# A decoder layer on one core: first stage with reordered weight loads and maxima, and the first chunk's input prepared in it

## The reference

```python
mod = silu(c) @ w_ada + b_ada                      # c: 9 rows (1 prompt, 8 samples); w_ada 1024 x 6144
sh1, sc1, g1, sh2, sc2, g2 = split(mod, 6)
h = rms_norm(x, norm1_w) * (1.0 + sc1) + sh1
proj = h @ w_in                                    # w_in 1024 x 4104
rq, rk, rv, rg, mq, mk, mv, mo, mi, mf = split(proj, ...)   # eight of 512 columns, two of 4
# retention over rq, rk, rv, gated by rg; mLSTM over mq, mk, mv, mo, mi, mf
x = x + g1 * (concat(y_r, y_m) @ w_out)
# then a second norm and a gated MLP with a causal convolution, and a last norm
```

## Time and profile before

| | |
|---|---|
| median of 3 runs | 2727.28 us (2724.01 to 2727.49) |
| the profiled execution's own time | 2726.41 us |
| its span | 2724.6 us |
| PE (TensorE matmul) busy | 2460.3 us, 90% |
| DVE (VectorE) busy | 1897.1 us, 70% |
| ACT (ScalarE) busy | 911.4 us, 33% |
| POOL (GpSimd) busy | 403.4 us, 15% |
| DMA | 279.87 MB, mean 103 GB/s |

### The profile page before, as it was taken

One profiled execution on the slowest core, in us unless ns is written; L12 is line 12 of the kernel. 1 busy time (PEld: TensorE's weight loads), 2 busy tenths in 40 slices (PEclk: granted clock), 3 DMA queues, 4 the chain that ended last, 5 costly groups with the idle time before them and its releaser, 6 DMA issues. The chain is left out here.

```text
span 2724.6 us, 44404 instructions
## 1 busy us (share of the span) xinstructions
PE 2460.3 (90%) x17028; PEld 1516.9 (56%) x17028; DVE 1897.1 (70%) x3889; ACT 911.4 (33%) x1371; POOL 403.4 (15%) x385
## 2 busy tenths in 40 slices
PE   2699999969999999599969999999999985899997
PEld 0355555557776777455536666666666652344443
DVE  6445565536888787568867777777777779967666
ACT  2324343314434444135432222222222224322222
POOL 0123222300000000012242212222122200000000
PEclk9999999979999999699989999999999997999999
DMA  9335434370242310433412221222122214333333
GB/s 258 105 112 163 149 122 135 102 247 33 86 147 85 141 71 15 131 117 111 134 50 73 79 74 49 75 76 74 61 66 72 78 63 159 112 94 103 107 89 93
DMA packets 197176, 279.87 MB, mean 103 GB/s; under 512 B 18840, under 2 KB 134088, under 8 KB 194876
## 3 DMA queue, kind: packets, MB, share of 16 engines
q1 hardware_dynamic: 197061, 278.35, 31.8%
HBM read 203.02 MB, written 75.29 MB: 102 GB/s over the span
## 5 line engine op out<-in xcount | busy, mean ns | idle before, releaser
L2510 PE MATMUL py<-h_parts,w_heads 128*128 128x384 f16 (+1 forms) x792 | 246.1, 311 | 19.1 <-DVE u_p L2667 19.1
L2511 PE MATMUL py<-h_parts,w_heads 128*128 128x384 f16 (+1 forms) x792 | 245.8, 310 | 0.0
L2512 PE MATMUL py<-h_parts,w_heads 128*128 128x384 f16 (+1 forms) x792 | 245.8, 310 | 0.0
L345 PE MATMUL prj<-w_heads,h_parts_t 128*128 128x512 f16 x512 | 196.2, 383 | 10.8 <-DVE h_parts_t L962 5.4
L346 PE MATMUL prj<-w_heads,h_parts_t 128*128 128x512 f16 x512 | 195.9, 383 | 0.0
L347 PE MATMUL prj<-w_heads,h_parts_t 128*128 128x512 f16 x512 | 195.6, 382 | 0.0
L345 PE MATMUL m_prj<-m_h,w_heads 128*128 128x128 f16 (+1 forms) x1088 | 179.5, 218 | 11.7 <-DMA m_h<-h_parts 10.3
L2510 PE MATMUL px<-h_parts,w_heads 128*128 128x384 f16 (+1 forms) x528 | 164.4, 311 | 17.5 <-PEq L1841 17.5
L346 PE MATMUL m_prj<-m_h,w_heads 128*128 128x128 f16 (+1 forms) x1088 | 179.4, 218 | 0.0
L347 PE MATMUL m_prj<-m_h,w_heads 128*128 128x128 f16 (+1 forms) x1088 | 179.4, 218 | 0.0
L345 PE MATMUL d_pm<-d_w,w_heads 128*128 128x512 f16 x392 | 152.0, 388 | 27.0 <-DVE w_heads L2373 27.0
(11 more groups left out here) (535 smaller groups left out, 6025.9 us busy)
## 6 DMA issues: line engine op xcount, KB each, us to landing
C_new<-in_w_up_dram SPq DMA_DIRECT2D x11, 2048.0 KB, 7.5
w_heads<-in_w_up_dram SPq DMA_DIRECT2D x44, 512.0 KB
d_a<-act_cols SPq DMA_DIRECT2D x174, 128.0 KB, 2.2
act_cols<-w_heads SPq DMA_DIRECT2D x44, 384.0 KB, 2.3
win_raw<-in_w_in_dram SPq DMA_DIRECT2D x8, 2048.0 KB, 14.6
win_raw<-in_w_ada_dram SPq DMA_DIRECT2D x8, 2048.0 KB
first_a<-in_w_down_dram SPq DMA_DIRECT2D x22, 512.0 KB, 3.9
wa<-in_w_ada_dram SPq DMA_DIRECT2D x4, 2048.0 KB, 18.0
```

What stands on the lines that cost most here:

```text
L345: nc.tensor.matmul(out, left[0], right[0], start=(k == 0), stop=False)
L2510: nc.tensor.matmul(out, left[0], right[0], start=(start and k == 0), stop=False, skip_group_check=True)
L2511: nc.tensor.matmul(out, left[0], right[1], start=False, stop=False, skip_group_check=True)
L2512: last = nc.tensor.matmul(out, left[1], right[0], start=False, stop=(k == KC // 2 - 1), skip_group_check=True)
```

## The change

In the first stage:

- The loads go into other buffers and another order. q, k go into a new tile `win_qk_raw`, v, g into `win_raw`; none is reused in the stage. Each load takes 128 rows of `w_in` by 1024 columns (512 KB), four of them (two row groups k) are a quarter. SyncE issues part 0 of `w_ada`, the gates, x, quarter 0, parts 1 to 3 (two `wa` buffers, so part i >= 2 waits until part i - 2 is used), quarters 1 to 3. Seven small loads move to ScalarE's queue.
- Maxima are taken quarter by quarter, four columns (q, k, v, g) at once; the blocks 1 to 4 share one spread and one set of six steps, after the last quarter.
- ScalarE copies the parts of `mod` out of PSUM; four partial rows are summed by the matmul that turns them (with `mod_fold`), and the bias is added to the columns.
- The first chunk's input is turned, multiplied and cut here. Block 1 is cut in two halves of rows (`cut_hi_halves`, `cut_lo_half`): both high halves and the first low half here.

In the second stage: the second low half and blocks 2 to 4 are cut; TensorE's first projection waits for the first low half, its middle for the second, each further projection for its block. `S_s` and the raw block for the next stage are loaded after the first late part instead of at the start, and that late part is loaded ahead of `step(1)`'s loads. Several tiles of the stage lie in the new raw buffer.

```diff
@@ class CutWeights @@
     def cut_hi(self, act, b):
         hi = self.blocks[b][1]
-        act.wait_ge(self.scaled, b + 1)
+        act.wait_ge(self.scaled, 2 if b else 1)
...
+    def cut_hi_halves(self, act, b):
+        act.wait_ge(self.scaled, 2)
+        for (raw, hi, _), done in zip(self.halves(b), (self.first_hi, self.hi_cut)):
+            self.nc.scalar.activation(hi, raw, ACT.Copy, scale=self.scale[:, b:b + 1]).then_inc(done, 1)
+
+    def cut_lo_half(self, dve, b, n):
+        raw, hi, lo = self.halves(b)[n]
+        if n == 0:
+            dve.wait_ge(self.first_hi, 1)
+        else:
+            dve.wait_ge(self.hi_cut, b + 1)
+        self.nc.vector.scalar_tensor_tensor(out=lo, in0=raw, scalar=self.scale[:, b:b + 1], in1=hi,
+                                            op0=ALU.mult, op1=ALU.subtract).then_inc((self.first_lo, self.lo_cut)[n], 1)
@@ phase_ada, sync @@
+            def load_quarter(q):
+                for k in (2 * q, 2 * q + 1):
+                    for raw, at in ((qk_raw, 0), (cut.raw, 2 * W)):
+                        sp.dma_start(raw[:, :, k * W:(k + 1) * W], win[:, k, at:at + 2 * W].rearrange("p (b n) -> p b n", n=W)).then_inc(w_in[q], 16)
...
+            load_part(0)
+            sp.dma_start(gates_raw[:].rearrange("p (k n) -> p k n", k=KC), cut.blocks[0][0], allow_slow_non_contiguous=True).then_inc(gates_in, 16)
+            core.norm1.load_x(sp, io["x_prompt"][0, 0:P], 0, P)
+            load_quarter(0)
+            load_part(1)
+            load_part(2)
+            load_part(3)
+            for q in range(1, 4):
+                load_quarter(q)
@@ phase_ada, tensor (after part 3 and turn_mod(1)) @@
+            pe.wait_ge(core.norm1.ready, 1)
+            for k in range(KC):
+                last = pe.transpose(tpx[:, k, :], core.norm1.xn[:, k * P:(k + 1) * P], core.ident[:])
+            last.then_inc(core.norm1.turned, 1)
+            spread.turn(pe, BOUND)
+            spread.turn(pe, HEADS)
@@ phase_ada, scalar @@
+            for i in range(EARLY):
+                act.wait_ge(wa_used, i + 1)
+                nc.scalar.copy(mrow[:, i], p_mod[:, i]).then_inc(mod_here, 1)
+            act.wait_ge(ab_here, 1)
...
+            nc.scalar.copy(core.h_parts[:, 0], core.h_full[:]).then_inc(core.h_hi, 1)
+            cut.cut_hi_halves(act, 1)
@@ phase_ret, sync @@
-            prep.load_raw(sp, 0)
-            sp.dma_start(S_s[:], io["state_ret"][0].rearrange("b h d e -> d b h e")).then_inc(s["state_in"], 16)
...
-            step(1)
             sp.wait_ge(cut.lo_cut, 5)
             load_late(0, 0, True)
+            sp.dma_start(S_s, io["state_ret"][0].rearrange("b h d e -> d b h e")).then_inc(s["state_in"], 16)
+            prep.load_raw(sp, 0)
+            step(1)
@@ phase_ret, tensor @@
-            for q in range(4):
-                if q == 0:
-                    turn_x(0, P)
-                if q == 3:
-                    pe.wait_ge(cut.lo_cut, 5)
+            pe.wait_ge(cut.first_lo, 1)
+            project(0, 0, P, cut.lo_cut)
+            for q in range(1, 4):
+                pe.wait_ge(cut.lo_cut, q + 2)
                 project(q, 0, P)
```

More of the change, by code:

```diff
@@ L245, in view, with set_scales @@
         return raw.rearrange("p (k n) -> p k n", n=n)
[L247 to L255, removed]
+    def set_scales(self, dve, top, first, n, steps):
+        at = slice(first, first + n)
+        power_of_two(self.nc, steps, top, self.scale[:, at], self.inv[:, at], self.bits[:, at])
+        dve.sem_inc(self.scaled, 1)
@@ L490, in _ @@
+        @block.scalar
+        def _(act):
             at = 0
@@ L498, in _ @@
[L498 to L529, removed]
-                    last = pe.transpose(col[:, q, k, :], mrow[:, 2 * q + k // 4, (k % 4) * P:(k % 4 + 1) * P], core.ident[0:NC9, 0:NC9])
-            last.then_inc(mod_turned, 1)
-            spread.turn(pe, BOUND)
@@ L555, in add_parts @@
-            def add_parts(i):
-                dve.wait_ge(wa_used, i + 1)
-                for t in range(4):
-                    ins = nc.vector.tensor_tensor(mrow[:, i], p_mod[NS * t:NS * t + NC9, i, :], mrow[:, i], ALU.add)
-                    if t < 3:
-                        steps.then(ins)
-                ins.then_inc(mod_here, 1)
-            cut.find_max(dve, 0, spread)
-            cut.set_scale(dve, 0, spread, steps)
-            dve.wait_ge(vecs_turned, 1)
+            nc.vector.tensor_copy(cT[:], p_c[:, :, 0:NC9])
@@ new lines, in _, with quarter_max @@
+            nc.vector.tensor_copy(c_wide[:, :, 0:NC9], p_c[:, :, 0:NC9]).then_inc(c_here, 1)
+            part_of = lambda t: core.ident[:, NS * t:NS * t + NC9]
+            steps.then(nc.vector.tensor_tensor(fold[:], part_of(0), part_of(1), ALU.add))
+            steps.then(nc.vector.tensor_tensor(fold[:], fold[:], part_of(2), ALU.add))
+            nc.vector.tensor_tensor(fold[:], fold[:], part_of(3), ALU.add).then_inc(c_here, 1)
+            def quarter_max(q):
+                dve.wait_ge(w_in[q], 64)
+                for n, raw in enumerate((qk_raw, cut.raw)):
+                    steps.then(nc.vector.tensor_reduce(tops[:, q, 2 * n:2 * n + 2], tile_of(raw, q), AX.X, ALU.max, apply_absolute_value=True))
@@ L570, in _ @@
+            cut.set_scales(dve, spread.fold(dve, GATES, steps)[:, 0:1], 0, 1, steps)
             cut.cut_lo(dve, 0)
-            for b in range(1, EARLY):
-                cut.find_max(dve, b, spread)
-                cut.set_scale(dve, b, spread, steps)
-                add_parts(b)
-                if b < 3:
-                    cut.cut_lo(dve, b)
-            dve.wait_ge(mod_turned, 1)
-            steps.then(nc.vector.tensor_copy(mod[:], col))
+            quarter_max(1)
+            dve.wait_ge(mod_turned, 3)
```

173 lines of the change are left out of this document (109 added, 64 removed).

## The result

| | before | after |
|---|---|---|
| median | 2727.39 us (2724.01 to 2727.82, 4 runs) | 2710.76 us (2708.41 to 2711.23, 4 runs) |
| the profiled execution's own time | 2726.41 us | 2711.22 us |
| its span | 2724.6 us | 2709.4 us |

The ratio is 0.9939, with a 95% interval from 0.9924 to 0.9954: faster, by 16.6 us or 0.6%. The forecast was 2710.0.

The account below looks back on a forecast made before the run. PE, busy 90% of the span, bounds the kernel outside its gaps; the first gap was the beginning. L 57.8, plus 12.6 to T 70.4, plus 24.2 put the turn at 94.6, 17.1 us earlier: 2710 us, range 2703 to 2723.

Parts of the forecast that it names:

- milestone: PE's turn of chunk 1's input, at 111.73 us before: forecast at 94.6, 17.1 us earlier, the kernel gaining the same.
- a quarter of `w_in`: First stage, load of 2 MB of `w_in` on SyncE's queue: taken as 7.5 us, between 4.8 and 11.0.
- gap ahead of part 3: SyncE's queue: the last part's load waits until part 1 is used, costing 0.7 us with the latency.
- L: Time when the last quarter of `w_in` has landed in the first stage: forecast 57.8 us.
- last quarter to projection: From L to T: maxima, scale steps, half cuts, barrier and handing over, 12.6 us.
- T: Time when PE begins to project, behind the barrier: forecast 70.4 us, against 88.11 before.
- T to the turn: Second stage, PE's projections beside the cuts on ACT and DVE: 24.2 us, with a 0.6 us wait at the end.
- rival A: First stage: DVE becomes the bound, with quarters at 4.8 us; 24.1 us gained, 2703 us; chance 12%.
- high end of a quarter: Slowest quarter load, 11.0 us: (8.9 + 13.1) / 2, with 13.1 from block 2 alone on the queue at 160 GB/s.
- DVE just in time: First stage: DVE finishes its earlier work at 57.4 us, before the last quarter lands at 57.8.
- Rival B: Reads of `w_in` stay slow, 11.0 us a quarter, DMA the bound; 3.1 us gained, 2724 us; chance 28%.
- Rival C: Sixteen short loads don't overlap in the queue, 3.9 us each; 15.3 us slower, 2742.6 us; chance 5%.

Follow-up runs that it names:

- second profile of the changed kernel: The changed kernel run again unaltered, beside the two reordered kernels on one chip: median 2708.97 us over 5 runs, ratio to before 0.9933.

## Why the prediction was right

The range, the sign and the milestone held. Of the mechanism, the part behind the last maximum held; what the forecast had release that maximum did not, and its hit to 1 us is in part luck. Step by step:

| step | forecast | measured |
|---|---|---|
| a quarter of `w_in` | 7.5 (4.8 to 11.0) | 5.4 |
| gap ahead of part 3 | 0.7 | 2.3, from the rates |
| last quarter landed, L | 57.8 | 55.66, in the run without quarter 2's maxima |
| DVE at the last quarter | 57.4 | 58.43 |
| last quarter to projection | 12.6 | 13.0 |
| T | 70.4 | 71.44 |
| T to the turn | 24.2 | 23.67 |
| turn of chunk 1 | 94.6 | 95.11 |
| gain | 17.1 | 16.6 at the turn, 15.2 in the span |

**The load's term was mis-sized twice.** A quarter took 5.4 us and not 7.5, which takes 8.4 off L for four. By my sum L would then be 49.4, rival A's country. It came at 55.66. Most of the difference is time that the sum left out, an estimate from the windows at the top: 1.9 us at 8 to 12 us (the bytes missing from 235 and 182 GB/s at a rate of 389), 2.3 at 28 to 32 instead of 0.7, three parts at 5.4 and not 5.2 (0.6), and 0.5 in 36:38 (287 GB/s). These make 4.6 of the 6.3. The other 1.7 I can't place. From 52 on the windows show what takes 1.1 us at full rate (1.3 in the run that has the landing at 55.66), so there is a tail of some 2.4 us between the last bytes and the release of DVE. The forecast's 10.2 for part 0 is such a release too and may hold the same tail; no run shows how much of it. The first dip stood in the trace of before as well, with 229 and 231 GB/s at 8:12; I did not read it.

Two readings under the high end of a quarter were off. Block 2 was not alone on the queue: the next part was issued 0.41 us behind it (20.26 and 20.67). And the 160 GB/s were one window of 2 us; over 26 to 36 us the rate was 181, which makes 11.6 us for a block and not 13.1. The seven small loads on ACT's queue delayed nothing: part 0's matmuls began at 10.27, where I had allowed 3 us.

**"DVE just in time" was the wrong side of a near tie.** The step that failed is that L releases the last maximum. I found DVE ready at 57.4 from quarter 2's landing at 50.3. In the trace it is counted from quarter 1's: 44.97, 4.64 for its maxima, 1.63 for the modulation, 4.64 for quarter 2, 2.55 for the factors' spread, together 58.43. (The forecast's own spacing has quarter 1 at 42.8, so it landed 2.2 us later than that.) The run without quarter 2's maxima shows the margin, 2.8 us. So rival A's mechanism was at work, though I had given it 12%, and its price of 24.1 us gained was wrong, because I had let the quarters be quick and everything else stay ideal. That the time was hit is luck in this step: L came 2.1 us sooner than forecast, DVE 1.0 us later, and the start of the last maximum, the later of the two, fell at 58.43 against 57.8.

**The 4 KB runs were no argument.** I took the low end of a quarter from "adjacent 4 KB", the high end from the distance of rows. The distance stayed, the runs of 2 KB were nearly as quick (368 and 374), and the rate was 389. What the runs separate is whether stripes of both kinds, here neighbours, are asked for close together. Rival B assumed that a stripe's rate carries over; it did not.

**Rival C, short loads.** Sixteen loads of 512 KB went through one queue; the last ones moved 389 GB/s (38 to 52 us), those of 256 KB 374 in the same stretch. The Trainium skill, DMA: Bandwidth & Descriptors, section Bandwidth, asks for 1 MiB or more; by the estimate made from its table, which was measured for loads issued by GpSimd, L would have been near 82. The traces here, of loads issued by SyncE, do not agree: L was 55.66.

**From T to the turn** the row by row sum held to 0.5 us, with a wait of 0.72 before project 1, where I had expected 0.6 before project 3. What my later expectations made of it was wrong: they held the last low cut for a fixed point, while in the run with block 1 cut whole it moved with the barrier, and the turn came 23.7 us behind T again. With the preparation behind the barrier it was 23.1.

**The clock.** The granted clock was 0.50 from 43 us to 75, so project 0 began at 1.2 GHz (a matmul each 0.43 us; from 75.65 on one each 0.22). PE was mostly idle from 46 us on, but the clock had fallen before that (1.00 in 36:38, 0.52 in 38:40, with PE at work). It cost nothing here: project 1 had to wait for its low cut anyhow. In the second profile of the changed kernel the slow stretch lasted until 77.4, the wait was gone, and the turn still came 23.7 us behind T.

## What to carry to other kernels

When two resources are forecast to be ready within a microsecond of each other, say which of them the trace must name as the releaser, and work out both from the same early landing. Then spend an experiment on removing one. A change that frees a queue is often limited next by the engine that consumes its loads: order its work by landing times, not by the program's logic, and give it waits as fine as the loads. When the work behind a barrier is a chain that starts there, each microsecond on the chain in front of it counts in full, and so does work that is moved from a hidden place ahead of it to the chain behind it.

## What the runs showed that I had not expected

Rows of `w_in` lie 16,416 bytes apart. A stripe of 512 columns read alone ran at 160 to 241 GB/s when it began at an odd multiple of 512 and at 270 to 395 at an even one, with the DMA engines busy for a share of 0.77 to 0.99 and of 0.89 to 1.08. Read with the neighbouring stripe in the same stretch of the queue, in loads of 256 or 512 KB and runs of 2 or 4 KB, both ran at 368 to 392. Why the odd ones are slower is open. Eight issues of 256 KB loads took SyncE 3.65 to 6.28 us in the kernel before with blocks split by k, where one of 2 MB took 0.37, so loads behind them on the queue start later (part 1 was issued at 14.00 us there, at 9.99 before).
